# The scores of the recurrent steps as 64x64 tiles of the array

## What is computed

```python
def _wkv_scan(r, w, kh, ak, v, kt, reverse):
    T, B, H, N = r.shape
    def step(S, inp):
        r_t, w_t, kh_t, ak_t, v_t, kt_t = inp
        sk = jnp.einsum('bhvk,bhk->bhv', S, kh_t)
        S = S * w_t[:, :, None, :] - sk[..., None] * ak_t[:, :, None, :] + v_t[..., None] * kt_t[:, :, None, :]
        return S, jnp.einsum('bhvk,bhk->bhv', S, r_t)
    S0 = jnp.zeros((B, H, N, N), jnp.float32)
    _, o = lax.scan(step, S0, (r, w, kh, ak, v, kt), reverse=reverse)
    return o
```

## Time and profile before

| what | before |
|---|---|
| median of three runs | 3314.43 us |
| lowest and highest run | 3310.67, 3314.73 us |
| span of the profiled execution | 3300.3 us |
| TensorE busy | 3197.5 us (97%) |
| TensorE weight loads busy | 2034.3 us (62%) |
| VectorE, ScalarE busy | 1787.4 us (54%), 1039.2 us (31%) |
| the recurrent stage, from the first step's state products to its end | 416.30 us |
| mean granted TensorE clock | 0.995 |

### The profile page before, as it was taken

One profiled execution on the slowest core, in us unless ns is written; L12 is line 12 of the kernel. 1 busy time (PEld: TensorE's weight loads), 2 busy tenths in 40 slices (PEclk: granted clock), 3 DMA queues, 4 the chain that ended last, 5 costly groups with the idle time before them and its releaser, 6 DMA issues. The chain is left out here.

```text
span 3300.3 us, 59856 instructions
## 1 busy us (share of the span) xinstructions
PE 3197.5 (97%) x25976; PEld 2034.3 (62%) x25976; DVE 1787.4 (54%) x2945; ACT 1039.2 (31%) x1588; POOL 142.8 (4%) x94
## 2 busy tenths in 40 slices
PE   9999999999999899989999999999999999999997
PEld 4564565555555555577887555567666666666665
DVE  2337762677777479146666332245645446545446
ACT  2336652334333223333433452003321111221111
POOL 0000000000000000000000000024200000200002
PEclk9999999999999999999999999999999999999998
DMA  3221101334543523365655223211112112122211
GB/s 140 58 71 36 46 23 60 118 122 139 167 155 121 193 74 139 122 186 168 177 167 147 89 76 149 91 51 64 58 64 81 61 64 83 58 93 74 70 64 64
DMA packets 218822, 328.53 MB, mean 100 GB/s; under 512 B 55488, under 2 KB 176704, under 8 KB 213440
## 3 DMA queue, kind: packets, MB, share of 16 engines
q1 hardware_dynamic: 218560, 324.69, 30.1%
HBM read 221.74 MB, written 96.34 MB: 96 GB/s over the span
## 5 line engine op out<-in xcount | busy, mean ns | idle before, releaser
L655 PE MATMUL ra_ps<-xT,ring 128*128 128x512 f32 (+1 forms) x1152 | 429.8, 526 | 0.0
L1891 PE MATMUL tl_ps<-merged,pool 128*128 128x320 f32 x1440 | 405.1, 434 | 2.5 <-PEq L108 1.8
L1891 PEld LDWEIGHTS tl_ps<-merged,pool 128*128 128x128 f32 x1440 | 273.6, 190 | 118.4 <-issue 4.0
L655 PEld LDWEIGHTS ra_ps<-xT,ring 128*128 128x128 f32 x1152 | 214.3, 190 | 199.0 <-issue 189.3
L2155 DVE TENSOR_TENSOR oR<-tl_ps,oR 128x320 f32<-128x320 f32 x416 | 202.1, 489 | 151.7 <-PE tl_ps L1891 148.9
L1106 PE MATMUL rg_ps<-xT,ring 128*128 128x512 f32 (+1 forms) x720 | 264.9, 523 | 3.3 <-PEq L108 3.3
L1976 ACT ACTIVATE ring<-tl_ps 128x320 f32<-128x320 f32 x96 | 42.0, 437 | 533.7 <-PE tl_ps L1891 533.7
L1106 PEld LDWEIGHTS rg_ps<-xT,ring 128*128 128x128 f32 x720 | 134.5, 191 | 113.9 <-issue 108.4
L1891 PE MATMUL tl_ps<-hold,pool 128*128 128x320 f32 x720 | 202.6, 432 | 0.0
L2161 DVE TENSOR_TENSOR merged<-tl_ps,ring 128x320 f32<-128x320 f32 x96 | 47.2, 491 | 255.5 <-PE tl_ps L1891 140.0
L1891 PE MATMUL tl_ps<-xT,pool 128*128 128x320 f32 x640 | 182.7, 432 | 0.0
(11 more groups left out here) (254 smaller groups left out, 4718.3 us busy)
## 6 DMA issues: line engine op xcount, KB each, us to landing
pool<-ub SPq DMA_DIRECT2D x320, 160.0 KB, 2.8
ub<-ra_ub SPq DMA_DIRECT2D x32, 1280.0 KB, 5.4
pool<-in_w_ff SPq DMA_DIRECT2D x32, 1024.0 KB, 4.8
pool<-in_w_ff SPq DMA_DIRECT2D x64, 512.0 KB, 3.4
ring<-in_w_in SPq DMA_DIRECT2D x38, 512.0 KB, 3.7
ub<-ra_v SPq DMA_DIRECT2D x16, 640.0 KB, 6.8
mg_gate<-gates SPq DMA_DIRECT2D x16, 640.0 KB, 3.9
xT<-in_xT SPq DMA_DIRECT2D x15, 640.0 KB, 8.6
```

The costliest lines, as they stand in the source:

```text
L655: last = pe.matmul(ps[:, bank + j, 0:n], w[c][:, 128 * i:128 * i + 128], xT[:, i, t0:t0 + n], start=(i == 0), stop=(i == KT - 1))
L1891: last = pe.matmul(bank(n, b), lhs(k), rhs(k), start=(fresh and k == 0), stop=(k == d - 1), skip_group_check=True)
```

## The change

In scores each matmul with 128 stationary columns is replaced by two with 64, one for each column half m: the first writes partitions 0 to 63 of the same bank, the second 64 to 127. The moving block, the banks, the semaphores and the waits stay as they are. The loops run j, then m, then h.

```diff
@@ -1307,10 +1307,11 @@
                     pe.wait_ge(masked, n - 1)
                     pe.wait_ge(kt_done, n - 1)
                 for j in range(2):
-                    for h in range(2):
-                        rows = slice(64 * h, 64 * h + 64)
-                        last = pe.matmul(ps[:, 4 + 2 * (q % 2) + h, 192 * j:192 * j + 192], x[rows, 2 * q + j, CH:3 * CH],
-                                         x[rows, 2 * q + j, 3 * CH:6 * CH], start=True, stop=True)
+                    for m in range(2):
+                        for h in range(2):
+                            last = pe.matmul(ps[half(m), 4 + 2 * (q % 2) + h, 192 * j:192 * j + 192],
+                                             x[half(h), 2 * q + j, CH + CH * m:2 * CH + CH * m],
+                                             x[half(h), 2 * q + j, 3 * CH:6 * CH], start=True, stop=True)
                 last.then_inc(sc_ready, 1)
```

## The result

The changed kernel takes 3345.89 us (median of four runs, 3344.36 to 3357.64) against 3312.55 us for the kernel before (four runs, 3308.01 to 3314.73). The ratio is 1.011, with a 95% interval from 1.0091 to 1.0128: slower by about 33 us. The forecast was 3344 us, with a range of 3298 to 3361.

The account below looks back on a forecast made before the run. TensorE was taken as bound by its instruction lines of some 253 records: 110.1 lines at 4.05 us make 446 us for the stage, +30 us with the -16 us gain contained; 3314.4 + 30 = 3344 us, range 3298 to 3361.

Parts of the forecast that it names:

- (a): scores(g+1, 1), between two 64x64 groups: 0.65 instead of 1.00 us, gain 0.35 us a step, -14 us.
- The rival with two by two: Four tiles don't stream side by side; scores calls take 8 rounds, some 80 us more, 3394 us; chance 0.04 (or anything worse).
- (b): scores(g+1, 0), between heads and the 32x32 group: only the first load shrinks, 0.04 us a step, -1.6 us.
- (c): scores(g+1, 2), between L1391 and heads: covered by VectorE's L1481, so 0, at most 0.03 us each.
- (d): scores(g+1, 3), between two heads: covered by the wait for X from L1527, so 0.
- the cover: At scores(g+1, 2) and (g+1, 3), VectorE's work sets the time, hiding the call unless scores grew past 0.9 us.
- (e): TensorE's instruction lines in the recurrent stage: 110.1 instead of 100, at 4.05 us each 446 us, +30 us.
- The cycle of 4.01 us: Time of one line where waits fall at two neighbouring line ends, seen twice in the trace of before.
- The even: Rival: a line's time falls to 3.7 to 3.85 us, result within 7 us of 3314; chance 0.10.
- faster case: Rival: lines keep up at 3.6 us, the gain of (a) and (b) stays, 3298 us; chance 0.18.
- The signs that were named: If right: 110 packets, issue waits well above 40 us, steps about 11.2 us, L1380 0.65 us after scores(g+1, 1).
- the 40 us in the prediction: Time lost in the stage before: 407.0 us for 39 steps against 367 us undisturbed, 1.0 us a step.

Follow-up runs that it names:

- q1: Kernel before with the column halves in the call scores(g+1, 1) alone: 3322.47 us against 3312.08 us, ratio 1.0039.
- b_less: Kernel before with the 32x32 products with nb (L1391) left out, 64 records a step less: 3276.57 us, ratio 0.9893.
- a_less: Changed kernel with the 32x32 products with nb (L1392) left out: 3309.65 us against 3314.89 us of the kernel before, ratio 0.9982.
- b96: Kernel before with each matmul of scores cut in two along the moving columns (2 x 96), no column halves: 3355.22 us, ratio 1.0131.

## Why the prediction was right

**(a) The gain of scores(g+1, 1)** was put at 0.35 us a step. Where no wait falls, the time up to the first L1381 record shows 1.94 - 1.63 = 0.31 us and the round behind it 0.10 - 0.06 = 0.04 us, together 0.35. The four tiles do stream 192 columns side by side: 4 rounds of 0.16 us. The rival with two by two is out.

**(b) scores(g+1, 0)**: 0.04 us was taken; from the first record of heads with SC to L1355 it is 1.88 us before and 1.84 us in the changed kernel, in the median step.

**(c) and (d)**: both 0, and so they were where no wait on issue falls. From the last L1391 record to the first of heads with Bs the median is 1.02 us in both kernels. From there to heads with KT the value that comes most often is 1.94 us in both; the median of the changed kernel is about 2.5 us, because waits on issue fall there in most of its steps. What I had not foreseen is how the cover works: in the new form the scores start while heads are still under way. In one step two records of scores start at 1644.30 us, and three further records of heads start behind them, the last at 1644.40. By its slices heads uses only two of the four quarters of the array, so these scores were probably in a quarter that it leaves idle; the trace does not name the quarter. It changes nothing, since NF and X set the time.

**(e) The lines** decided, as said. The number was right: 10 more packets in the 39 steps. That the size came out so close is luck, two errors that cancel. I took 4.05 us for a line; the stage of the changed kernel, from 1426.40 us to the end of its last heads at 1886.98, has 460.6 us and 110 lines, 4.19 us each. That is 15 us more than my 446. The cycle of 4.01 us that I leaned on stood on two cases. The changed kernel has 17 lines with a wait at both ends, and they take 3.50 to 5.06 us, with a median of 4.24: the cycle is no constant, and my two cases were short ones. On the other side I set the sum against a profiled execution of before of 3300.3 us and put the 14.1 us up to the median down to what lies around the span. The runs of the changed kernel show that only 1.8 us lie around it (3347.10 us with a span of 3345.3); the rest was that the profiled execution of before, with 3302 us by the same sum, was some 10 us faster than its median, and faster than every one of the runs of before on record. A more usual one would have had more than 4.15 us a line, about 4.25 us if the 10 us lay in this stage (an estimate). So the term is +44 us between the two profiled executions, where I had +30, and +33 us between the medians.

**Which rival was near.** The even and the faster case hung on the lines coming every 3.8 us or sooner. The trace of before held what speaks against it, the two cycles of 4.01 us with a wait at both ends. The gaps of 0.10 us before and after the scores went away with the change of form, and by the rule that was weighed against it, of the Trainium skill (TensorEngine Tiling, Key Properties), a change of the tiling mode drains TensorE; the trace agrees with the rule (the scores start 0.06 instead of 0.16 us after the pair of products with S before them), but not with the result that follows from it alone.

**The signs that were named.** 110 packets in the stage came; waits on issue rose from 27 to 72 us (the 40 us in the prediction were worked out from the steps, and the profile names 27 of them); a step takes 11.57 us where 11.2 were named; L1381 starts 0.65 us after the scores; and 16 records of scores take 0.83 us.

## What to carry to other kernels

Where many small matmuls follow each other, count the instructions as well as their durations: the page gives the packets of the instruction queue, and records divided by packets is the length of a line. If waits on "issue" lie inside groups of equal instructions, at distances that are multiples of that length, the stage runs at the rate of its lines. Then a change that saves array time but adds instructions can lose (14 us saved and 10 us lost in q1), and one that removes instructions can gain more than their own duration (36 us for 15 in b_less).

## What was not expected of the hardware

**The time of this stage is nearly independent of TensorE's work in the kernels tried.** Between a_less and b96 the busy time differs by 70 us; the time for a line is 4.17 and 4.19 us. I had expected the own work to show at least in b96, whose undisturbed step would be 9.5 + 0.8 = 10.3 us.

**The clock falls after the waits.** In the 39 steps of the profiled execution of before the granted clock is 1.00 throughout; in the changed kernel its mean is 0.97, because seven stretches, 24 us in all, fall to the lower of the two levels, 1.2 GHz. In the 3.1 us ahead of each of them TensorE had been busy for 1.2 to 1.6 us. One lies in the window from 1529.10 to 1532.50 us that is shown with the result, with a mean of 0.55. Ahead of it TensorE had been busy for 1.16 of 3.10 us, with a wait at a line end of 1.94 us:

```profile
1526.00:1529.10 3.10, 1.16 (x56) 0.92 (x52) 0.30 (x2) 0.87 (x2) 0.00 (x0) 0.94 0.50 149
```

```profile
1528.57 0.35 PE L1392 MATMUL rc_ps<-rc_nb,rc_Wt 32*32 32x32 f32 x12 [1.94 <-issue]
1528.85 1.56 PE L1312 MATMUL rc_ps<-pool 64*64 64x192 f32 x16
```

The 16 records of scores that follow take 1.56 instead of 0.88 us. No run separates how much of the 33 us this is, but the record bounds it. Over the whole execution the granted clock was 0.988 to 0.991 in the four runs of the changed kernel and 0.992 in the median of the 33 later runs of before (0.990 to 0.995). The difference of about 0.0025, of 3346 us, is some 8 us (an estimate, of all the time in which the clock was lower). So it can't be the main part, and a_less with two such stretches (7 us) and b_less with none have the same time for a line as the changed kernel with seven.
